# Seven buffers for gathered expert rows in place of eight, a third weight block kept, and 24 more experts added by VectorE

## The reference, cut to what matters

```python
q = (xc @ w_q).reshape(PEER_CHUNK, PEER_HEADS, 2, PEER_HALF)
sc = jnp.einsum('chid,hikd->chik', q, sub_keys)
top_s, top_i = lax.top_k(sc, PEER_TOPK)
...
expert = i1 * PEER_KEYS + i2
gate = jax.nn.softmax(best_s, axis=-1)
u_e = jnp.take(u_tab, expert, axis=0)
v_e = jnp.take(v_tab, expert, axis=0)
act = jax.nn.gelu(jnp.einsum('chkd,cd->chk', u_e, xc))
return jnp.einsum('chk,chkd->cd', (gate * act), v_e)
```

## Time and profile before

| | us |
|---|---|
| median of 3 runs | 1755.75 (1753.16 to 1757.75) |
| the profiled execution | 1753.23 |
| its span, first to last instruction | 1751.5 |
| PE busy | 1595.6 (91%) |
| DVE busy | 1205.4 (69%) |
| ACT busy, POOL busy | 596.1, 591.8 |
| moved by DMA | 680.39 MB, 388 GB/s over the span |
| granted TensorE clock, mean | 0.982 of full speed |

### The profile page before, as it was taken

The page is one execution under the profiler, slowest core; times in us unless marked ns, Lnnn a source line. Parts: engine busy times, 40 slices in busy tenths (PEclk is TensorE's granted clock), DMA queues, the critical chain, the costliest instruction groups (busy, mean ns, idle before and its releaser), DMA issues.

```text
span 1751.5 us, 19654 instructions
## 1 busy us (share of the span) xinstructions
PE 1595.6 (91%) x6652; PEld 971.0 (55%) x6652; DVE 1205.4 (69%) x3334; ACT 596.1 (34%) x1445; POOL 591.8 (34%) x527
## 2 busy tenths in 40 slices
PE   7999999999999999998989989999999987777777
PEld 7878866545547777644645646644655643222232
DVE  7721489985886567997557567998657566667665
ACT  4132232463334232264323233255323232222222
POOL 0000143444333323443333433444433434333432
PEclk9999999999999999999999999999999999999999
DMA  9436599999999999999999999999999989999996
GB/s 380 192 145 272 222 376 421 418 388 421 421 416 396 422 421 421 421 421 418 420 422 400 416 421 420 421 373 402 421 421 420 419 355 422 421 421 422 421 422 288
DMA packets 94580, 680.39 MB, mean 388 GB/s; under 512 B 10488, under 2 KB 10768, under 8 KB 12304
## 3 DMA queue, kind: packets, MB, share of 16 engines
q0 software_dynamic: 73728, 536.90, 74.5%
q1 hardware_dynamic: 20752, 142.23, 20.0%
HBM read 678.05 MB, written 1.05 MB: 388 GB/s over the span
## 4 chain that ended last, share of the span: by engine, by line
PE 37%; DMA 30%; DVE 12%; ACT 4%; issue 2%; DVEq 0%; ACTq 0%
DMA slots<-expert_rows,expert 30%; PE bank L771 21%; PE bank L388 8%; DVE slots L1606 5%; PE bank L556 3%; PE bank L756 1%; ACT diag L1191 1%; DVE sg L1229 1%; PE bank L759 1%; DVE att L1483 1%; DMA ring<-w_blocks 1%; DVE coef L1229 1%; PE bank L699 1%; DVE x L1229 0%; ACT L1204 0%
## 5 line engine op out<-in xcount | busy, mean ns | idle before, releaser
L771 PE MATMUL bank<-slots,diag 128*128 128x512 f32 x1916 | 912.5, 613 | 124.3 <-ACT diag L1191 119.8
L880 POOL DMA_INDIRECT slots<-expert_rows,expert x512 | 589.9, 1152 | 1136.3 <-PE bank L771 878.3
L1606 DVE CUSTOM_DVE_ANT_0 slots<-slots,htok 128x1024 f32<-128x1024 f32 x512 | 626.4, 1223 | 356.2 <-DMA slots<-expert_rows,expert 352.5
L771 PEld LDWEIGHTS bank<-slots,diag 128*128 128x128 f32 x1916 | 349.7, 194 | 541.7 <-issue 325.2
L1204 ACT ACTIVATE gel<-dot 128x2 f32<-128x2 f32 (+1 forms) x257 | 52.4, 204 | 697.4 <-DVE dot L1606 693.3
L388 PEld LDWEIGHTS bank<-hT,ring 128*128 128x128 f32 x1696 | 205.8, 193 | 48.0 <-issue 47.2
L1191 ACT ACTIVATE diag<-ident,coef 128x128 f32<-128x128 f32 x479 | 168.1, 394 | 186.4 <-DVE coef L1229 183.1
L388 PE MATMUL bank<-hT,ring 128*128 128x128 f32 x1696 | 206.6, 276 | 2.5 <-DMA ring<-w_blocks 2.5
L1229 DVE SCALAR_TENSOR_TENSOR coef<-gel,ginv,gexp 128x2 f32<-128x2 f32 (+1 forms) x257 | 54.2, 211 | 54.2 <-ACT gel L1204 50.2
L1204 ACT ACT_TABLE_LOAD x65 | 83.4, 1283 | 1.2
L1229 DVE SCALAR_TENSOR_TENSOR sg<-pad,prm,sg 128x128 f32<-128x128 f32 x240 | 71.6, 343 | 0.0
(11 more groups left out here) (274 smaller groups left out, 1516.9 us busy)
## 6 DMA issues: line engine op xcount, KB each, us to landing
ring<-w_blocks SPq DMA_DIRECT2D x99, 1024.0 KB
slots<-w_blocks SPq DMA_DIRECT2D x23, 1024.0 KB, 7.6
slots<-expert_rows,expert POOLq DMA_INDIRECT x512
kept<-w_blocks SPq DMA_DIRECT2D x4, 1024.0 KB, 13.3
keys<-w_blocks SPq DMA_DIRECT2D x2, 1024.0 KB, 10.7
prm<-small SPq DMA_DIRECT2D x2, 768.0 KB
x<-x_rows SPq DMA_DIRECT2D x2, 512.0 KB, 10.9
slots<-mem_rows SPq DMA_DIRECT2D x1, 1024.0 KB, 7.5
```

What stands on the lines that cost most here:

```text
L771: last = mm(bank[h][:, :], diag[:, i % DIAGS, :], slots[:, n % SLOTS, D + h * 512:D + (h + 1) * 512], start=m == 0, stop=n == end)
L880: nc.gpsimd.indirect_dma_start(slots[:, n % SLOTS, :], None, experts_d, bass.IndirectOffsetOnAxis(ap=idx[q % 2][:, k:k + 1], axis=0),).the ...
L1606: v.tensor_tensor_reduce(out=slots[:, s, 0:D], in0=slots[:, s, 0:D], in1=htok[:, ph % 2, :], scale=1.0, scalar=0.0, op0=ALU.mult, op1=ALU.add,
```

## The change

One slot less (`SLOTS` 7) and one kept block more (`STAY` 3: h2 as well), which need the same memory. The first stage's wide ring shrinks to eight places (`WIDE`), and the first stage has 34 blocks that aren't kept (`EARLY`). So h2 is loaded once for each layer in place of twice, and two loads of 1 MB go. In the two middle expert stages (`n` 128 to 383) DVE also adds every fourth expert at places 64 to 111, twelve in each: 57 in place of 33. The old pattern keeps its period of eight. The memory rows' second load stays ahead of the second stage's first `wq` load.

```diff
-EARLY = 35
-WIDE = 9
-
-STAY = 2
-SLOTS = 8
+EARLY = 34
+WIDE = 8
+
+STAY = 3
+SLOTS = 7
...
-TAKER = ["vector" if (n < 16 or 104 <= n < 144) and n % SLOTS in (2, 4, 7)
-         or n < NG - PER and 44 <= n % PER < 60 and n % 4 == 2 else "tensor" for n in range(NG)]
+TAKER = ["vector" if (n < 16 or 104 <= n < 144) and n % 8 in (2, 4, 7)
+         or n < NG - PER and 44 <= n % PER < 60 and n % 4 == 2
+         or PER <= n < NG - PER and 64 <= n % PER < 112 and n % 4 == 2 else "tensor" for n in range(NG)]
...
-                if n == FIRST["wq"] + 2 and stage == 1:
+                if n == FIRST["wq"] + STAY and stage == 1:
```

## The result

The changed kernel takes 1765.78 us in the median of six runs (1762.0 to 1772.5) against 1756.27 us of the kernel before: a ratio of 1.006, 95% interval 1.0048 to 1.0072; the medians lie 9.5 us apart. Measured again later, beside other kernels, it gave 1.0072 (1.0052 to 1.0092), with medians 10.9 us apart. The forecast was 1761.7 us in a range of 1750 to 1768: the side was right, and the change of +5.9 us was 3.6 us too small (5.0 us by the second measurement).

A forecast was written before the change was run, and what follows sets the result against it. The DMA at 421 GB/s was taken as the bound; seam +2.5, slot costs at 345, 755, 1150, 1425 us, less 2.8 at 940 us and 2.5 at 1330 us, gave +5.9: 1761.7 us, range 1750 to 1768 us.

The forecast's parts named there:

- The ledger of the DMA: After the first 205 us, the end comes when all bytes have moved at 421 GB/s, plus the DMA's idle time.
- turns at 345, 540, 940, 1150, 1425: Places (us) where the path turns from an engine back to the DMA; a missing slot costs one transfer, 2.5 us, each.
- 755: Stretch 755 to 800 us: DVE late but the DMA lost only 0.2 us; bounds 0 and 2.5, half taken, +1.2 us.
- two loads less: Loads of h2 dropped near 500 and 1330 us: 2.5 us of DMA time saved at each, 5.0 us together.
- the seam: Around 205 us: three weight loads (7.5 us) move among the gathers, 5.0 us of idle gets filled: +2.5, bounds -5 and +7.5.
- moved experts: 24 experts from PE to DVE: pay only at 940 to 970 us, removing 2.8 us idle and a 2.5 us slot cost.
- the pace stays, and I take 0 for all saturated stretches: Where the DMA is the bound, seven slots leave 10.4 us from issue to dot against 5.75 us needed: cost 0.
- 500 to 560 us: One turn at 540 to 560 us, +2.5, offset by the first layer's dropped h2 load, -2.5: 0, bounds -2.5 and +2.5.
- 1150 and 1425 us: DVE's late stretch and the seam to the last stage: +2.5 us each for the missing slot, the last called surest.
- turns are free: Rival: DMA fills lost time with weight blocks at each turn, only bytes count: -7.8, 1748.0 us; chance 0.14.
- PE stays late at 940 us: Rival: PE still busy 30 of 30 us at 940 to 970 us, total 12.5 us slower, 1768.3 us; chance 0.14.
- some issues are held: POOL's gather issues held by DVE instructions; added additions could cost at most 2.6 us more at 940 to 970 us; left at 0.

The follow-up runs named there:

- 1.0102: Kernel before, eight slots, but from expert 16 on each gather also waits for the expert seven back, so seven are in use: 1.0102 (1.0079 to 1.0124), 17.9 us slower.
- 1.0085: Changed kernel with DVE's 24 added experts back on PE, still seven slots and three kept blocks: 1.0085 (1.0068 to 1.0102) to the kernel before.
- second profile: Profile of the unaltered changed kernel from its later measurement beside other kernels: ratio 1.0072 (1.0052 to 1.0092) to the kernel before, profiled span 1761.3 us.
- the seam undone: Changed kernel with the first stage's wide ring started six places further on: 1.0066 (1.0049 to 1.0082), timed again 1.0061 (1.0043 to 1.008), to the kernel before.

## Why the prediction was right, and where its size was off

The ledger of the DMA was the right view. The bytes fell, PE's work fell, and the time rose by idle time of the DMA, mostly in the stretches that it named. Set against the runs, regrouped by cause:

| cause | forecast, us | measured, us |
|---|---|---|
| seven slots, everywhere | +13.7 (turns at 345, 540, 940, 1150, 1425: 12.5; 755: 1.2) | +17.9 |
| two loads less, with the seam | -5.0 + 2.5 = -2.5 | -3.0 (1.0102 to 1.0085) |
| moved experts, given seven slots | -2.8 - 2.5 = -5.3 | -2.3 to -4.4 |
| sum | +5.9 | +10.5 (second time +12.6) |

Each measured entry is the step from one run's ratio to the next, so they add up to the changed kernel's ratio by themselves and don't check it. Of the steps only the first is clear of noise: the interval of 1.0102 overlaps that of 1.0085, so 3.0 us for the two loads is an estimate. The 17.9 us come from a kernel with eight slots of which seven are used, and no run has seven slots and nothing else changed.

**The slot.** This is the mis-sized term. The price of one turn was about right. Where the dots of one stretch are timed in all profiles, those with seven slots are apart from those with eight:

| dots of experts | eight slots, us | seven slots, us | means apart | forecast |
|---|---|---|---|---|
| 40 to 84 (345 us) | 132.8 to 135.2 | 135.7 to 137.2 | 2.1 | 2.5 |
| 272 to 330 (1150 us) | 180.1 to 181.7 | 181.6 to 183.7 | 1.9 | 2.5 |
| 392 to 396 (1425 us) | 8.8 to 9.1 | 11.1 to 11.6 | 2.3 | 2.5 |

These are seven profiles with eight slots (one of them with seven for experts 84 to 127 only) and six with seven. What was wrong is the step "the pace stays, and I take 0 for all saturated stretches", with its 4.7 us to spare. Both of its numbers came from the best case. A slot is held 7.0 us after its dot in the last stage: from dot to the issue of the next gather into the slot the trace of before has 6.9 us in the median there, but 10.0 us over experts 16 to 383, where mixer work lies over the gathers, and up to 18.3 us. One example is the slot of expert 92, held 14.6 us from its dot to the gather of expert 100, which waits 5.39 us for PE:

```profile
494.71 1.22 DVE L1606 CUSTOM_DVE_ANT_0 slots<-slots,htok 128x1024 f32<-128x1024 f32 x1
...
509.33 0.94 POOL L880 DMA_INDIRECT slots<-expert_rows,expert  x1 [5.39 <-PE bank L771]
```

The other number, 5.75 us, is a gather into an empty queue; with other gathers under way the median landing was 8.7 us in the run of six slots. From issue to dot the last stage has 10.8 us in the changed kernel (forecast 10.4), which still covers that, and no loss shows there in the second profile. But the shortest such time in experts 84 to 103 fell from 10.5 to 7.2 us and in 104 to 127 from 9.9 to 7.8 us (9.2 and 7.8 us in the second profile), so there it no longer does. Six slots should by the same step still have kept pace (7.9 us over 5.75 us) and ran at 376 GB/s. A rate of 421 GB/s didn't tell whether the queue had two slots to spare or a tenth of one. Of the idle time that six slots add in the profile (92.7 us over 200 to 1720 us) 28.7 us lie in the last stage, and the rest is spread over nearly all the others. How it divides between holds and landings is open; no run separates them.

**500 to 560 us.** I took one turn, "against which the second stage's missing load of h2 stands". There are two dry places, with the DMA as the bound between them, and over 450 to 600 us they grew by 5.5 and 5.8 us in the two profiles. The missing load buys less than 2.5 us there: leaving out both loads with eight slots gave 1.8 us together.

**1150 and 1425 us.** The last was called the surest, and it was: by the dots 2.3 us in the mean, and seen in all six profiles with seven slots, though the DMA's idle time grew by 1.2 us in one profile of the changed kernel and 2.4 us in the other. At 1150 us the dots come 1.9 us later, while the idle time is no sign of it: over 1100 to 1250 us it is 6.9 to 8.5 us in the profiles with eight slots and 6.8 to 7.9 us in those with seven. The kernel before has the least of the first, so its single profile is a poor base there. Why the two readings differ at 1150 us is open.

**The seam.** Orders and times came as forecast (SP after 217 us, gather 6 before 215 us). The gap was filled as forecast too. The first two rows are of before, the last two of after:

```profile
200.00:210.00 10.00, 10.00 (x92) 10.00 (x91) 6.02 (x27) 3.60 (x8) 3.69 (x4) 1.00 0.64 227
210.00:235.00 25.00, 22.43 (x135) 18.00 (x134) 17.50 (x45) 11.49 (x24) 9.77 (x10) 0.88 0.86 332
...
200.00:210.00 10.00, 10.00 (x92) 10.00 (x92) 6.56 (x29) 3.78 (x9) 3.76 (x4) 1.00 0.29 93
210.00:235.00 25.00, 21.29 (x141) 16.57 (x139) 16.73 (x44) 11.40 (x25) 8.66 (x10) 1.00 1.01 421
```

From 210 us on the idle time fell from 5.3 us to nothing. But in 200 to 210 us it rose by 3.2 us, mostly because the third block, which moved there before, was no longer in the queue; so over 200 to 235 us the idle time fell by 2.1 us. The net price in the ledger is 5.0 us for the 2.1 MB that no longer move ahead of 200 us, less 1.3 us idle in 200 to 300 us: +3.7 us (second profile +2.8), against +2.5. Lateness at expert 12 was 3.9 us (second profile 2.9). Alone, with eight slots, it costs about 1.6 us. With seven it can't be told from none.

**The moved experts.** The mechanism is seen in the windows at both places. With seven slots they pay 2.3 to 4.4 us; alone they gave 1.0001. The 2.8 us that the forecast took off at 940 us was what one profile of the kernel before had lost, and other profiles with eight slots lost 0.9 to 2.1 us there.

**Luck.** Part of the nearness of the sum is luck. The growth forecast where seven slots were taken for enough was too small by 2.6 to 3 us twice (450 to 600 and 600 to 850 us), and the idle time at 1100 to 1250 us and the tail took 1.5 and 1.7 us off again, for which the forecast had no reason.

**The rivals.** That turns are free fell with the run of seven slots in use. That PE stays late at 940 us didn't happen. That some issues are held was right, and the trace tells by what. Of the 174 gathers of before that POOL issued during a dot, 152 took over 1.0 us, and all 13 issued during an addition to `x` did. All but one of these 165 ended 0.80 to 0.83 us after the DVE instruction's end. Of the 155 issued while no DVE instruction ran none took over 0.95 us. The issue of 1.62 us at 217.32 us is one, begun in this dot:

```profile
216.90 1.23 DVE L1606 CUSTOM_DVE_ANT_0 slots<-slots,htok 128x1024 f32<-128x1024 f32 x1 [1.07 <-DMA slots<-expert_rows,expert]
```

The port rule of the Trainium skill ("SBUF — State Buffer", "Who interferes with whom") says that a DVE instruction with two SBUF inputs contends with a GpSimd one that reads SBUF; both the dot and the addition have two such inputs, and the trace agrees. The 24 more additions cost nothing by it that shows: 17 issues in place of 13 fell into an addition, and the mean issue went from 1152 to 1130 ns.

## What to carry to other kernels

A transfer ring's depth can't be judged from a DMA that runs at its full rate; take the smallest margin over all stages, for instance by making the kernel wait for one slot fewer without changing anything else. Take how long a buffer is held from the stage that holds it longest, and the landing time from a busy queue. Count the price of a buffer as about one transfer at each place where the bound passes from an engine back to the DMA (1.9 to 2.3 us here for a transfer of 2.49 us), and expect places that were only just covered to join. Bytes saved paid here only where PE could follow (1.8 us of 5.0 us, not certain, with PE as the bound beside one of them), so try a saved load together with work taken off the late engine.

## What the runs showed of the hardware that was not expected

Six executions of the changed kernel spread over 10.5 us (1762.0 to 1772.5) and six more over 12.6 us, where six of the kernel before spread over 4.6 us (1753.16 to 1757.75) and 29 later ones over 8.7 us. And one profile could lie 5 us from the next of the same kernel (1756.4 and 1761.9 us with the seam undone). With 1 MB gathers of 2.49 us, the step from eight to seven usable slots cost 17.9 us and the step from seven to six 78.6 us more. A gather's issue on POOL that begins during a DVE dot or addition lasts until about 0.8 us after that instruction ends (164 of the 165 issues over 1.0 us in the kernel before): 1.45 us in the mean during a dot against 0.94 us.
